# A macaron encoder block on one core: token halves around the seams, and real tiles where dummy products stood

## What is computed

```python
x = x + 0.5 * g1 * swiglu(modulate(rms_norm(x, norm_ffn1), sh1, sc1), w_gate, w_up, w_down)
x = x + g2 * token_mixing(modulate(rms_norm(x, norm_mix), sh2, sc2), ...)
x = x + 0.5 * g3 * swiglu(modulate(rms_norm(x, norm_ffn2), sh3, sc3), w_gate, w_up, w_down)
return rms_norm(x, final_norm)
```

## Time and profile before

| | us |
|---|---|
| median of 3 runs (lowest, highest) | 1182.09 (1180.71, 1185.41) |
| profiled execution, its own time | 1180.76 |
| its span, first to last instruction | 1179.1 |
| TensorE busy | 1157.2 (98%) |
| VectorE busy | 617.9 (52%) |
| ScalarE busy | 474.9 (40%) |
| GpSimd busy | 59.2 (5%) |

### The profile page before, as it was taken

How to read it: one execution, slowest core, us unless ns; L and a number is a source line. 1 busy time by engine, 2 the same in 40 slices (tenths; PEclk the granted TensorE clock), 3 DMA queues, 4 the chain that set the end, 5 groups by cost and what they waited for, 6 DMA issues and landing times.

```text
span 1179.1 us, 15623 instructions
## 1 busy us (share of the span) xinstructions
PE 1157.2 (98%) x5446; PEld 961.9 (82%) x5446; DVE 617.9 (52%) x999; ACT 474.9 (40%) x708; POOL 59.2 (5%) x83
## 2 busy tenths in 40 slices
PE   8999999999999989999999999998999999999997
PEld 7888888888888868888888888886888888888886
DVE  4766666665555566665565566746333333333332
ACT  5132332332222266555555566434443443422222
POOL 3301000000000002000011110000000000000000
PEclk9899999999999999999999999999999999999999
DMA  9567566556555315332343442331333333333332
GB/s 313 154 201 249 183 215 206 167 196 204 161 167 169 104 53 136 99 97 72 89 113 95 115 116 72 93 103 54 97 99 89 106 89 100 95 89 95 97 98 85
DMA packets 221142, 151.34 MB, mean 128 GB/s; under 512 B 5078, under 2 KB 202916, under 8 KB 221108
## 3 DMA queue, kind: packets, MB, share of 16 engines
q1 hardware_dynamic: 217252, 139.02, 39.5%
q0 software_dynamic: 3280, 9.79, 3.1%
q10 hardware_dynamic: 576, 2.10, 0.5%
HBM read 148.73 MB, written 4.52 MB: 130 GB/s over the span
## 4 chain that ended last, share of the span: by engine, by line
PE 64%; issue 32%; DVE 2%; ACT 1%; DMA 1%; ACTq 0%; DVEq 0%; POOLq 0%; POOL 0%
PE bank L1238 18%; PE bank L1240 18%; PE bank L1239 18%; PE bank L1451 1%; PE bank L1361 1%; PE bank L1439 1%; PE bank L1444 1%; PE bank L1467 1%; PE bank L1466 1%; DMA xin<-in_x_dram 1%; PE bank L1269 1%; DVE hL L893 0%; PE bank L1278 0%; PE bank L1535 0%; PE bank L1345 0%
## 5 line engine op out<-in xcount | busy, mean ns | idle before, releaser
L1238 PE MATMUL bank<-hH,wH 128*128 128x512 f32 x1080 | 425.4, 394 | 6.3 <-DVE hL L893 5.1
L1240 PE MATMUL bank<-hH,wL 128*128 128x512 f32 x1080 | 421.6, 390 | 0.0
L1239 PE MATMUL bank<-hL,wH 128*128 128x512 f32 x1080 | 421.4, 390 | 0.0
L567 ACT ACTIVATE wH<-raw 128x1024 fp32r<-128x1024 f32 (+1 forms) x187 | 194.8, 1042 | 532.6 <-PE bank L1240 532.6
L806 DVE TENSOR_TENSOR wL<-raw,wH 128x1024 fp32r<-128x1024 f32 (+1 forms) x187 | 224.7, 1202 | 313.0 <-ACT wH L567 312.3
L1238 PEld LDWEIGHTS bank<-hH,wH 128*128 128x128 f32 x1080 | 203.1, 188 | 53.3 <-DVE hL L893 5.9
L1240 PEld LDWEIGHTS bank<-hH,wL 128*128 128x128 f32 x1080 | 203.0, 188 | 42.7
L1239 PEld LDWEIGHTS bank<-hL,wH 128*128 128x128 f32 x1080 | 203.2, 188 | 40.6
L1238 PE MATMUL bank<-actH,wH 128*128 128x512 f32 x352 | 137.3, 390 | 0.0
L1240 PE MATMUL bank<-actH,wL 128*128 128x512 f32 x352 | 137.2, 390 | 0.0
L1239 PE MATMUL bank<-actL,wH 128*128 128x512 f32 x352 | 137.2, 390 | 0.0
(11 more groups left out here) (166 smaller groups left out, 976.5 us busy)
## 6 DMA issues: line engine op xcount, KB each, us to landing
adaw<-in_ada_w_dram SPq DMA_DIRECT2D x28, 1024.0 KB, 6.0
raw<-in_ffn_w_gate_dram SPq DMA_DIRECT2D x43, 512.0 KB, 3.9
raw<-in_ffn_w_up_dram SPq DMA_DIRECT2D x43, 512.0 KB, 3.8
raw<-in_mix_w_in_dram SPq DMA_DIRECT2D x41, 512.0 KB, 3.9
raw<-in_ffn_w_down_dram SPq DMA_DIRECT2D x32, 512.0 KB, 3.7
adas<-in_ada_w_dram SPq DMA_DIRECT2D x16, 512.0 KB, 8.1
raw<-in_ffn_w_down_dram SPq DMA_DIRECT2D x16, 384.0 KB, 3.3
raw<-in_mix_w_out_dram SPq DMA_DIRECT2D x8, 512.0 KB, 3.7
```

Source lines behind the costliest of these rows:

```text
L567: nc.scalar.activation(wH[s][:, :n * P], raw[s][:, :n * P], ACT.Copy).then_inc(hi_done, 1)
L1238: T.matmul(o, a[0], b[0], start=start, stop=False)
L1239: T.matmul(o, a[0], b[1], start=False, stop=False)
L1240: return T.matmul(o, a[1], b[0], start=False, stop=stop)
```

## The change

1. **Last tile of a down projection, last three tiles of the output projection.** They are made for tokens 0 to 255 first, then for 256 to 511 (`last_down`, `to_ffn`), as products of 256 columns, so that x, its squares and the norm of the first half can be had while TensorE works on the second. The weights are kept for both: some units get other homes in memory (`HOME`).
2. **The units behind a seam** (f, q and k of the first pair; the first four of FFN 2) are made by halves too (`part`), with tiles of several units taken in turn, and with sums, squares and spreads between them. All dummies of the seams are gone. `two_units` is gone; v of the first pair is one unit of full width in its own bank.
3. **At the start** block 0 of units 2 and 3 stands in place of the second 20 dummies.
4. **The first pair of heads.** q and k's copies come first, then `forget_exp`, the copy of v, `forget_logs`; `forget_sums` is at the pair's end.
5. **The output.** The first 256 tokens are turned, scaled and sent while the last tile's second half is made; the last transfer of the left half of channels is issued by ScalarE.

Apart from unit homes, every product of before is there, 372 of them as two halves.

TensorE at the first seam, before: sums (L1345), squares (L1352, L1355), dummies (L1361) and spread (L1368), in this order.

The core of the diff (the same halves on ScalarE and VectorE are left out):

```diff
+        HOME = {U_FA - 3: (pair_of(hH, 6), pair_of(hL, 6)), U_FA - 2: (pair_of(hH, 4), pair_of(hL, 4)),
+                U_FA + 2: (wH_y[1][:, :], wL_y[1][:, :]), U_FA + 3: (ptH[:, :UT * P], ptL[:, :UT * P]),
+                U_END - 3: (pair_of(hH, 6), pair_of(hL, 6)), U_END - 2: (pair_of(hH, 4), pair_of(hL, 4)),
+                U_OUT + 6: (wH_x[0][:, :], wL_x[0][:, :]), U_OUT + 7: (wH_x[1][:, :], wL_x[1][:, :]),
+                U_GU2 + 1: (wH_y[0][:, :], wL_y[0][:, :]), U_GU2 + 2: (wH_y[1][:, :], wL_y[1][:, :])}
+        def home(u):
+            return HOME[u] if u in HOME else regular(u)
...
-                dummies(20)
+                tiles(2, 0)
+                tiles(3, 0)
                 tiles(0, 1)
                 tiles(1, 1)
-                tiles(2, 0)
                 tiles(2, 1)
                 first_parts(2)
                 first_sums(2)
-                tiles(3, 0)
                 tiles(3, 1)
                 tiles(0, 2)
                 tiles(1, 2)
...
+            def part(u, b, tiles, q, e):
+                pe.wait_ge(lo_done, u + 1 + FREE)
+                wh, wl = home(u)
+                for t in tiles:
+                    pe.wait_ge(hL_done, q * DT + t + 1)
+                    cols = slice(t * P, (t + 1) * P)
+                    ins = three(bank[:, b, HALF[e]], (wh[:, cols], wl[:, cols]), (hH[:, t, HALF[e]], hL[:, t, HALF[e]]),
+                                t == 0, t == DT - 1)
+                return ins
+            def half_squares(m, e, q):
+                if m != 1:
+                    pe.wait_ge(ssqa_done[m], DT - 1 + START)
+                else:
+                    pe.wait_ge(ssqh_done, 2 * e + 2)
+                if e:
+                    pe.wait_ge(ms_done, q)
+                ts = range(e * TT // 2, (e + 1) * TT // 2)
+                for t in ts:
+                    T.matmul(bank[:, B_SSQ, t:t + 1], ssqa[:, t * P:(t + 1) * P], ones[:, 0:1], start=t == ts[0], stop=False)
+                pe.wait_ge(sqh_done[m], (e + 1) * (1, 3, 1)[m])
+                for t in ts:
+                    ins = T.matmul(bank[:, B_SSQ, t:t + 1], tmp[:, 1, t * P:(t + 1) * P], ones[:, 0:1], start=False, stop=t == ts[-1])
+                ins.then_inc(ssq_ps, 1)
+            def half_spread(q, e):
+                pe.wait_ge(diag_done, q + 1)
+                for t in range(e * TT // 2, (e + 1) * TT // 2):
+                    ins = T.matmul(bank[:, B_BC[e], t * P:(t + 1) * P], ones[:, :], diag[:, t, :], start=True, stop=True)
+                ins.then_inc(bc_done, 1)
...
+            def last_down(m, u0):
+                i, u6, u7 = DT // 2 - 1, u0 + 3 * DT - 6, u0 + 3 * DT - 3
+                q = (1, 3, N_NORMS - 2)[m]
+                pe.wait_ge(x_done[m][0], i + START)
+                for k in range(3):
+                    k0, cnt = PARTS[k]
+                    pe.wait_ge(lo_done, u6 + k + 1 + FREE)
+                    for n in range(cnt):
+                        ins = three(bank[:, 5, :], tile((u6 + k) % 2, n), (actH[:, k0 + n, :], actL[:, k0 + n, :]),
+                                    k0 + n == 0, k0 + n == FT - 1)
+                    ins.then_inc(unit_done, 1)
+                def some(k, tiles, e, start, stop):
+                    wh, wl = home(u7 + k)
+                    for n in tiles:
+                        f = PARTS[k][0] + n
+                        cols = slice(n * P, (n + 1) * P)
+                        ins = three(bank[:, B_DOWN[e], HALF[e]], (wh[:, cols], wl[:, cols]), (actH[:, f, HALF[e]], actL[:, f, HALF[e]]),
+                                    start and n == tiles[0], stop and n == tiles[-1])
+                    return ins
+                pe.wait_ge(x_done[m][1], i + START)
+                for k in range(3):
+                    pe.wait_ge(lo_done, u7 + k + 1 + FREE)
+                    ins = some(k, range(PARTS[k][1]), 0, k == 0, k == 2)
+                ins.then_inc(half_done[m], 1)
+                pe.wait_ge(x_done[m][0], i + 1 + START)
+                some(2, range(0, 3), 1, True, False)
+                half_squares(m, 0, q)
+                some(2, range(3, 6), 1, False, False).then_inc(unit_done, 1)
+                if m == 2:
+                    for t in range(TT // 2):
+                        turned_out(0, t, range(4))
+                    for t in range(TT // 2):
+                        turned_out(1, t, range(4))
+                some(1, range(UT), 1, False, False).then_inc(unit_done, 1)
+                if m == 0:
+                    half_spread(1, 0)
+                some(0, range(UT), 1, False, True).then_inc(unit_done, 1)
+            def to_mix():
+                f, q, k = (U_FA, B_FA), (U_FA + 1, 0), (U_FA + 2, 1)
+                for t in range(0, DT, 2):
+                    part(*f, (t, t + 1), 1, 0)
+                    last_sums(range(2 * t, 2 * t + 2))
+                    part(*q, (t, t + 1), 1, 0)
+                    if t == 2:
+                        half_squares(0, 1, 2)
+                    ins = last_sums(range(2 * t + 2, 2 * t + 4))
+                ins.then_inc(ada_sum, 1)
+                part(*k, range(0, 4), 1, 0)
+                half_spread(2, 1)
+                part(*k, range(4, DT), 1, 0)
+                for t in (0, 2):
+                    for ub in (f, q, k):
+                        part(*ub, (t, t + 1), 2, 1)
+                for ub in (f, q, k):
+                    part(*ub, range(4, DT), 2, 1).then_inc(unit_done, 1)
+                pe.wait_ge(lo_done, U_FA + 4 + FREE)
+                wh, wl = home(U_FA + 3)
+                for t in range(DT):
+                    cols = slice(t * P, (t + 1) * P)
+                    ins = three(bank[:, B_V, :], (wh[:, cols], wl[:, cols]), (hH[:, t, :], hL[:, t, :]), t == 0, t == DT - 1)
+                ins.then_inc(unit_done, 1)
...
+            def to_ffn():
+                u4 = U_OUT + 4
+                pe.wait_ge(x_done[1][0], 2 + START)
+                h_unit(u4, u4 % 2, bank[:, 0, :]).then_inc(unit_done, 1)
+                def some(n, tiles, e):
+                    wh, wl = home(u4 + 1 + n)
+                    for t in tiles:
+                        cols = slice(t * P, (t + 1) * P)
+                        ins = three(bank[:, B_OUT[e][n], HALF[e]], (wh[:, cols], wl[:, cols]), (hH[:, t, HALF[e]], hL[:, t, HALF[e]]),
+                                    t == 0, t == DT - 1)
+                    return ins
+                pe.wait_ge(x_done[1][1], 2 + START)
+                for n in range(3):
+                    pe.wait_ge(lo_done, u4 + n + 2 + FREE)
+                    some(n, range(DT), 0).then_inc(half_done[1], 1)
+                some(0, range(0, 4), 1)
+                half_squares(1, 0, 3)
+                some(0, range(4, DT), 1).then_inc(unit_done, 1)
+                some(1, range(0, 4), 1)
+                half_spread(3, 0)
+                some(1, range(4, DT), 1).then_inc(unit_done, 1)
+                pe.wait_ge(xh_done[1], 4)
+                some(2, range(DT), 1).then_inc(unit_done, 1)
+                def units(us, tiles, e):
+                    for u in us:
+                        ins = part(U_GU2 + u, u, tiles, 3 + e, e)
+                        if e and tiles[-1] == DT - 1:
+                            ins.then_inc(unit_done, 1)
+                units((0, 1, 2), (0, 1), 0)
+                units((0, 1, 2), (2, 3), 0)
+                half_squares(1, 1, 4)
+                units((0, 1, 2), (4, 5), 0)
+                units((3,), range(0, 6), 0)
+                half_spread(4, 1)
+                units(range(N_FIRST), (6, 7), 0)
+                for t in (0, 2):
+                    units(range(N_FIRST), (t, t + 1), 1)
+                for u in range(N_FIRST):
+                    units((u,), range(4, DT), 1)
...
+                        made = first and pp == 0
                         for k, dst, sc in ((0, qHH, SCALE), (1, kHL, 1.0)):
-                            prep(u0, 10, i, k0 + k + 2)
+                            if not made:
+                                prep(u0, 10, i, k0 + k + 2)
                             act.wait_ge(s_done, g * 8 + START)
                             act.wait_ge(unit_done, i * 10 + u0 + k0 + k + 1)
                             for other in range(2 - k):
                                 for h in range(2):
                                     nc.scalar.activation(dst[head_rows(h ^ other), h, :], bank[head_rows(h), k, :], ACT.Copy,
                                                          scale=sc).then_inc(qhi, 1)
-                            if first and pp == k == 0:
-                                forget_logs()
+                        if made:
+                            forget_exp()
+                            prep(u0, 10, i, k0 + 3)
                         act.wait_ge(unit_done, i * 10 + u0 + k0 + 3)
-                        nc.scalar.activation(vT[:, :], bank[:, 0, :], ACT.Copy).then_inc(v_copied, 1)
```

(27 more changed lines are left out.)

501 lines of the change are left out of this document (336 added, 165 removed).

## The result

| | before | after |
|---|---|---|
| median (lowest to highest, 6 runs each) | 1182.95 (1180.71 to 1185.41) | 1171.38 (1169.90 to 1172.83) |
| ratio, 95% interval | | 0.990 (0.9882 to 0.9918) |
| profiled execution, its own time | 1180.76 | 1172.53 |
| its span | 1179.1 | 1170.8 |
| mean granted clock | 0.992 | 0.988 |

The forecast was 1172.5, range 1165 to 1179. The time is right, and so is the mechanism of the seams, of the end and of the new stall. But in the profiled execution the start has the wrong sign, and the clock's fall behind the stall is missing from the sum: 4.2 us together. The terms for waits and restarts and the tail were too careful, by 3.6. That the time lies so near is partly luck.

A forecast was written before the change was run, and what follows sets the result against it. TensorE was taken as the bound nearly everywhere. Terms -0.8 - 10.2 - 9.0 - 1.75 + 5.0 + 1.8 + 3.4 + 1.7 + 1.0 gave -8.9: 1171.9 from 1180.76, set at 1172.5 us towards the median; range 1165 to 1179.

The forecast's parts named there:

- the clock's fall: Rival: the first pair's stall also costs the clock, or seam handovers cost more; with dearer halves +5, 1177.5 us; chance 22%.
- Halves, +5.0: 744 products of 256 columns replace 372 of 512, at 0.12 us each: +5.0 us (0 to +23.6).
- Restarts, +1.0: More waits are checked and some stop weight loads from running ahead: +1.0 us (0 to 2).
- Start, -0.8: At the start, 12 products of units 2 and 3 replace 20 dummies: -0.8 us (0 to -1.4).
- Seam 1: FFN 1 to the mixer: dummies and waits on TensorE go, -10.2 us, before the price of what replaces them.
- +1.8 of new waits: In the first seam, TensorE's waits around the spread, f's tile 7 and the first squares: +1.8 us.
- First pair, +3.4: First pair of heads: TensorE idles before the turned probabilities, as logarithms precede unit 73's weight copy: +3.4 us (0 to 4).
- Seam 2 and end: Output projection to FFN 2: -9.0 us of waste, +1.7 new waits; at the end, a shorter tail: net -1.75 us.
- Dear halves: Rival: loads and half products don't fit in 0.12 us; at the scores' 0.145 the kernel takes 1191 us; chance 6%.
- unhidden loads: Rival: weight loads don't overlap at all, half products cost 0.188 us or more, kernel 1223 us; chance 2%.
- The covered stall: Rival: the first pair's idle on TensorE is hidden, 3.4 us less, 1169 us; chance 10%.
- The seams gain nothing: Rival: VectorE's chain in the seams is as long as before, only start and end gain, 1180 us; chance 5%.

The follow-up runs named there:

- logs late: Changed kernel with the forget gate's logarithms behind ScalarE's last step of the first pair and four last sums behind the second pair's `qL`: 1167.02 us, 0.9853 of before.
- clock held: Changed kernel with 26 dummy products ahead of the first turned probabilities, timed to end with the stall: 1169.94 us, 0.9871 of before.
- run 1: The changed kernel again with no edit, in a later series: 1169.89 us, 0.9876 of before.
- 12: The changed kernel a third time with no edit, in another series: 1171.78 us, 0.9906 of before.
- quarters: Changed kernel with 720 whole products of both down projections made as four products of 128 columns each: 1328.24 us, 1.1225 of before.
- 4: Changed kernel with the old start: 20 dummies in their old place, block 0 of units 2 and 3 back behind: 1171.13 us, 0.9883 of before.
- 11: Changed kernel with the first half's 16 turned output tiles behind the last product: 1170.41 us, 0.9894 of before.
- halves: Changed kernel with 720 whole products of both down projections made as 1440 products of 256 columns: 1179.32 us, 0.9977 of before.
- slow norm, run 9: Changed kernel with VectorE making every scaled tile of both seams twice, the extra one into free memory: 1184.60 us, 1.0011 of before.
- run 5: Changed kernel with only the weight copy of unit 73 moved ahead of the forget gate's logarithms on ScalarE: 1165.93 us, 0.9857 of before.
- run 6: Changed kernel with logarithms behind ScalarE's last step of the first pair and all forget sums ending VectorE's second pair: 1173.52 us, 0.9924 of before.

## Why the prediction was right, step by step

- **Halves, +5.0: right.** 0.12 in both seams (in seam 1 behind 252 of 276 halves the next product starts 0.12 later) and 0.120 over long rows. The scores' 0.145 is not a price of 256 columns.
- **Restarts, +1.0: measured near nothing.** A first product behind sums or a spread takes 0.20 instead of 0.12, some 17 times. But the first one-column record stands only 0.03 ahead of the second, 0.08 under its 0.111, and that gives it back. From 409.73 to 410.30 four sums and a half pass in 0.57, which is 4 x 0.111 + 0.12:

```profile
409.73 0.50 PE L1610 MATMUL bank<-ones,adac 128*128 128x1 f32 x4
410.10 0.36 PE L1489 MATMUL bank<-hH,wH 128*128 128x256 f32 x1
410.30 0.28 PE L1490 MATMUL bank<-hL,wH 128*128 128x256 f32 x1
```

- **Start, -0.8: right on average as far as three traces of the old order tell, wrong in the trace read first.** The twelve products ran at 0.43 and ended at 37.69, as worked out (37.7). But A came 0.75 later than in before, and the clock was at half once more, from 44.6 to 51.4. The two other traces with such a fall (logs late, clock held) have A within 0.2 of that; runs 1 and 12 have none, and come 0.6 and 0.7 ahead of before.
- **Seam 1: -10.2 and its price, net -6.2; measured -7.6.** (-10.2 + 1.8, 276 of the halves for 138 wholes +1.85, restarts 0.4.) The mis-sized terms are the +1.8 of new waits and the restarts. The two waits of 0.3 cost 1.1 by the distances around them (0.57 and 0.53 where 0.12 is normal, and the products behind), the restarts nothing, which leaves 0.3 unplaced; I had taken a pair at 2.0, it costs 1.87.
- **First pair, +3.4: right mechanism, right size, one consequence missing.** The order of ScalarE's queue told it. The prediction set the clock's fall apart as a rival with a chance of 22%; it belonged in the sum: with the stall alone B to C is 132.9, in after and in quarters it is 2.8 more, in runs 1, 4, 11 and 12 1.6 more. In halves and slow norm the stall left the clock up (B to C 132.9), so the fall is likely, not certain.
- **Seam 2 and end, together -5.3; measured -7.5.** (-9.0 + 1.7 - 1.75, 468 halves for 234 wholes +3.1, restarts 0.6.) One wait of 0.56 in seam 2 for the 1.7 I had counted, restarts that cost nothing for 0.6, and a tail half a us shorter than forecast make some 2 of the 2.2. (The 2.65 in front of the last product is short by 0.1: 24 records at 0.115 are 2.76.)
- **Sum.** Forecast -0.8 - 6.2 + 3.4 - 5.3 = -8.9; measured +0.75 - 7.60 + 6.08 - 7.53 = -8.3. Start and clock were 4.2 worse, seams and end 3.6 better.
- **Rivals.** Dear halves and unhidden loads are out (7, 8). The Trainium skill's rule that a load overlaps a running product only where the row groups differ ("TensorE: Matmul & The Clock Gate", The mechanism), which the prediction priced, is contradicted by both: full 128 x 128 loads with half products pass in 0.120 each, with quarters in 0.111. The same section of that page also lets a load into the background weight buffer run ahead, and with that case the runs agree. The covered stall did not come; run 5 shows what it would have taken. "The seams gain nothing" is out for this kernel, but only 0.8 us of VectorE per pair away: in run 9 A to B is 359.65, for 359.33 before, 3.4 of it by the clock.

**The version that beats both** is copy first: 0.9857 (0.983 to 0.9883) of before, by one statement moved. Logs late is its equal within the intervals. In B to C they are 4.0 and 4.1 below run 1; by whole times the interval of copy first still overlaps that of run 1 (0.986 to 0.9893), which ran in another series.

## What to carry to other kernels

When a change reorders an engine's queue, walk down that queue to the next thing that *another* engine waits for: here four short operations ahead of one weight copy cost about a third of what the change could win, and moving the sums "where there is room" (run 6) cost more than that through a third engine. Price an idle of TensorE as the idle and what the clock may take behind it. Compare kernels by stretches between events that both traces have: one such stretch repeats within 0.05 us in nearly all traces where whole times of the changed kernel scatter by 5.
